# Delta rule of a hybrid block: N and A formed from the raw channel-major keys, the key scale folded into the decay tile

## The chip, the cores and the metric

The kernel runs on one core of one Trainium2 chip. The metric is the device time of one execution in microseconds. The kernel before took 1391.35 us, the median of 3 runs (1386.46 to 1392.39).

## The reference, cut to what matters

One layer on x of 1024 tokens by 1024 channels, all in float32. After an rmsnorm and one projection, two mixers work side by side: forgetting attention (FoX, 8 heads of 64) and a gated delta rule (GDN, 4 heads of 128). Their outputs are joined, projected by w_out, normed and added; a squared-relu MLP of width 4096 follows. The part that the change touches is the delta rule:

```python
cq = cq * lax.rsqrt(jnp.sum(cq * cq, axis=-1, keepdims=True) + EPS) * GDN_HEAD_DIM ** -0.5
ck = ck * lax.rsqrt(jnp.sum(ck * ck, axis=-1, keepdims=True) + EPS)
beta = jax.nn.sigmoid(gb)
decay = exp(where(incl, gc[..., :, None] - gc[..., None, :], -inf))
m = where(strict, einsum("bhncd,bhnkd->bhnck", k * beta, k) * decay, 0.0)
t_inv = triangular_solve(eye + m, eye, lower, unit_diagonal)
u = t_inv @ (v * beta)
w = t_inv @ (k * beta * exp(gc))
a_intra = einsum("bhncd,bhnkd->bhnck", q, k) * decay
# then a scan over the chunks: v_new, o, and the new state
```

## The kernel before, in words

The kernel has three parts one after the other: the input projection with its causal convolutions, the mixers, and w_out with the MLP. The change lies in the mixers.

For each of the 4 delta-rule heads p there is a preparation (`list_prep`) and a scan over 8 chunks of 128 tokens (`list_scan`). The FoX heads are cut in 64 tiles of 128 queries (`list_fox`), whose items lie between those of the delta rule on every engine. A preparation works on two halves g (0 and 1) of 4 chunks each. Its steps are "fills": each fill is one PSUM bank of four 128x128 blocks written by TensorE, either by four transposes (`four_turned`) or by four products (`four_products`), and then read by ScalarE or VectorE. The fills of all heads rotate through 3 banks (`NFILL_BANKS`), so that a fill can't begin before the fill three places ahead of it has been read.

The keys come from DRAM channel-major (`c_raw["k"]`, `c_first["k"]` for head 0: 128 channels by 1024 tokens). The path of the keys of one half before the change is:

1. fill "k": TensorE turns the raw keys to token-major in PSUM.
2. ScalarE squares them (L1815), VectorE sums (L2349) and adds the epsilon (L2351): "mean". GpSimd raises the mean to a power (L2864), for the values.
3. VectorE forms `k_scale` = beta / mean (L2362, L2364) and writes the scaled keys `kn` = keys * `k_scale` (L2366): "scale". Then it writes `kbg` (L2375) from the same bank: "kb". `kbg` has one buffer for each half, so "kb" of head p waits for the fill "W" of head p-1, which reads it.
4. fill "knT": TensorE turns `kn` back to channel-major; ScalarE copies it to `knT` (L1841).
5. fill "N": products of `knT` with the raw keys; VectorE multiplies by -1 and the decay tile (L2448) into `n_low`. fill "A": products of `knT` with the raw queries, times the decay tile (L2452), into `a_t`.
6. When both halves of `n_low` are there, the SyncE queue gathers the 16x16 diagonal blocks through DRAM (L1454, L1457), VectorE inverts them ("lane", L2388 to L2427), the queue scatters them back (L1462 on), and three levels of fills X, TX and XR build the inverse. Fills W and U multiply it into the keys and the values, and the scan of the head can begin.

The decay tile (128 by 1024 floats) is made for each head: a broadcast load of the gate row (L1364), two ScalarE reads of it (L1796, L1797), a GpSimd product with the mask (L2869), and 8 ScalarE exponentials (L1803). The next head's row is loaded once both N and both A have been read. GpSimd also makes `kd` (L2879, from `kn`), `qdT` (L2885), `z_tok` (L2918), the powers of the norms (L2903, L2905), and for each FoX tile `q_lo` (L2895), which the scores of that tile wait for.

The order of the items on each engine is worked out before the kernel is built, by `plan()`: a list scheduler in plain Python that has a cost for every item (`pe_cost`, `act_cost`, `dve_cost`, `pool_cost`, `sp_cost`), what each item follows (`fill_follows`, `dve_follows`, `pool_follows` and so on) and a fixed beginning (`BEGUN`). It always takes the item that can start first, and of those that start together the one with the longest way to the end. On the chip each engine works its list off in order. An item added or taken out can so move many others on all five engines. The planner lets a fill start only when the other things its reader waits for are done.

Of the kernel before, what the change touches and what calls it, by code (L numbers as in the profile page):

```python
# [14 lines left out]
P = 128  # L15
# [15 lines left out]
LEVELS = 7  # L31
# [59 lines left out]
ACT_READS = ("mask", "fv", "z", "knT", "W")  # L91
# [30 lines left out]
def list_prep(p):  # L122

    fills = [(p, what, g, 0) for what in ("fv", "k", "q", "v", "z", "knT", "N", "A", "W", "U") for g in range(2)]
    fills += [(p, "XR", g, BASE - 1) for g in range(2)]
    for lev in range(BASE, LEVELS):
        for g in range(2):
            fills += [(p, "X", g, lev), (p, "XR", g, lev)] + ([(p, "TX", g, lev)] if lev < LEVELS - 1 else [])
    for name in fills + [(0, "mask", 0, 0)] * (p == 0):
        what, lev = name[1], name[3]  # L130
        to("pe", "fill", name)
        if what in ("k", "q"):
            to("act", "square", name)
            to("dve", "mean", name)
            if what == "k":
                to("pool", "power", name)
                to("dve", "scale", name)
                to("dve", "kb", name)
        else:
            to("act" if read_by_act(what, lev) else "dve", "read", name)  # L140
        if what == "knT":
            to("pool", "kd", name)
    to("act", "gl", p)
    to("pool", "decay", p)
    to("act", "decay", p)
    to("pool", "qd", p)
    to("pool", "z", p)
    to("sp", "gather", p)
    to("sp", "scatter", p)
    for part in range(LANE_PARTS):  # L150
        to("dve", "lane", p, part)
    if p >= 1:
        for what in ("fv", "k", "q", "v", "z", "g"):
            to("sp", "load", what, p)
# [81 lines left out]
def pe_cost(item):  # L236

    kind = item[0]
    if kind == "fill":
        what, lev = item[1][1], item[1][3]  # L240
        if what == "mask":
            return 0.33
        return 0.44 if what in ("fv", "k", "q", "v", "z", "knT") or (what == "XR" and lev < LEVELS - 1) else 0.9
    if kind == "scores":
        blocks = FOX_TILES[item[1]][2] + 1
        return 0.066 + sum(2 * max(0.112, 0.057 * min(4, blocks - b)) for b in range(0, blocks, 4))
    if kind in ("turn", "pv"):
        return (0.11 if kind == "turn" else 0.224) * blocks_of(*item[1:])
    return 0.224 if kind == "scan_v" else 0.672 if item[2] else 0.448
# [25 lines left out]
def pool_cost(item):  # L275

    return {"power": 1.02, "decay": 2.37, "kd": 1.05, "qd": 2.37, "queries": 0.47, "z": 2.4, "tail_power": 1.02, "w_out": 2.37}[item[0]]
# [40 lines left out]
def fill_follows(p, what, g, lev):  # L318

    before = [reader((p, w, g, l)) for w, l in {  # L320
        "N": [("knT", 0)], "A": [("knT", 0)], "X": [("TX", lev - 1)] * (lev > BASE), "TX": [("X", lev), ("XR", lev - 1)],
        "XR": [] if lev < BASE else [("TX", lev)] if lev < LEVELS - 1 else [("X", lev), ("XR", lev - 1)],
        "W": [("XR", LEVELS - 1), ("k", 0)], "U": [("XR", LEVELS - 1), ("v", 0)]}.get(what, [])]
    if what in ("fv", "z", "k", "q", "v"):
        before.append(("sp", "load", what, p))
    elif what == "A":
        before.append(("sp", "load", "q", p))
    elif what == "knT":
        before += [("dve", "scale", (p, "k", g, 0))] + [fill(p - 1, "A", g, 0)] * (p >= 1)
    elif (what, lev) in (("X", BASE), ("XR", BASE - 1)):  # L330
        before += [("sp", "scatter", p)] + [fill(p - 1, w, g, 0) for w in "WU"] * (p >= 1)
    elif what == "X" or (what == "XR" and lev < LEVELS - 1):
        before.append(fill(p, "TX", g, lev - 1 if what == "X" else lev))
    return before + [fill(p, what, 0, lev)] * (g if what in ("fv","k","q","z","v") else 0)


def pe_follows(kind, n, c=0):

    if kind == "fill":
        return fill_follows(*n)  # L340
    if kind == "scores":
        return [("pool", "queries", n)] + [("dve", "k_lo", n // NT)] * (n % NT == 0) + [("dve", "max", n - 1)] * (n >= 1)
    if kind == "turn":
        before = FOX_CHUNKS[max(FOX_CHUNK[(n, c)] - 1, 0)]
        return [("act", "exp", n)] + [(copied_by(*before), "copy") + before] * ((n, c) != (0, 0))
    if kind == "pv":
        before = [(copied_by(n, c), "copy", n, c), reader((FOX_TILES[n][0], "fv", 1, 0))]
        return before + ([("pe", "pv", n, 0)] if c else [("act", "out", n - 1)] * (n >= 1))
    if kind == "scan_v":
        return [("dve", "state", n, c - 1), ("act", "o", n, c - 1), reader((n, "W", c // HT, 0)), reader((n, "U", c // HT, 0))]  # L350
    before = [reader((n, w, c // HT, 0)) for w in "UA"] + [("pool", "qd", n), ("pool", "kd", (n, "knT", 1, 0))]
    if c:
        return before + [("dve", "v_new", n, c)] + [("pe", "scores", NT - 1)] * ((n, c) == (0, NCHUNK - 1))
    return before + last_state(n - 1) + [("act", "o", n - 1, NCHUNK - 1)] * (n >= 1)


def act_follows(kind, n=None, c=0):

    if kind == "square":
        p, what, g, _ = n  # L360
        if what == "k":
            return [fill(*n)] + [("pool", "kd", (p - 1, "knT", g, 0))] * (p >= 1)
# [33 lines left out]
def dve_follows(kind, n, c=0):  # L396

    if kind in ("mean", "scale", "kb"):
        p, what, g, _ = n
        if kind == "mean":  # L400
            return [("act", "square", n)] + [("dve", "read", (p - 1, "v", g, 0)), ("dve", "scale", (p - 1, "k", g, 0))] * (what == "k" and p >= 1)
        return [("dve", "mean" if kind == "scale" else "scale", n)] + [fill(p - 1, "W", g, 0)] * (kind == "kb" and p >= 1)
    if kind == "lane":
        return [("dve", "lane", n, c - 1) if c else ("sp", "gather", n)]
    if kind == "read":
# [4 lines left out]
        elif what in ("N", "A"):  # L410
            before += [("act", "decay", p)] + ([fill(p - 1, "X", g, LEVELS - 1)] * (p >= 1) if what == "N" else last_state(p - 2))
# [27 lines left out]
def pool_follows(kind, n):  # L439
# [5 lines left out]
    if kind == "kd":  # L445
        return [("dve", "scale", (n[0], "k", n[2], 0)), fill(*n)] + last_state(n[0] - 2)
# [7 lines left out]
def sp_follows(kind, what, n=0):  # L454
# [12 lines left out]
    return [fill(n - 1, {"k": "N", "q": "A"}.get(what, what), 1, 0)] + [("pool", "qd", n - 1)] * (what == "q")  # L467
# [99 lines left out]
POOL_PREP = numbered_of("pool", "power", "decay", "kd", "qd")  # L567
# [115 lines left out]
def build(nc, x, pre_mix_norm, w_in, fox_f_bias, fox_out_norm, gdn_conv_w, gdn_a_log,  # L683
# [7 lines left out]
    with ExitStack() as ctx:  # L691
# [124 lines left out]
        knT = [placed(f"knT{g}", at, [P, 4, P]) for g, at in enumerate((192448, 206784))]  # L816
# [468 lines left out]
        def _(sp):  # L1285
# [60 lines left out]
            def load_c(kind, h):  # L1346
                if h >= 1:
                    sp.wait_ge(filled, FILL[(h - 1, {"k": "N", "q": "A"}.get(kind, kind), 1, 0)])
# [272 lines left out]
        def _(act):  # L1621
# [184 lines left out]
            def square(name):  # L1806
# [5 lines left out]
                if what == "k":  # L1812
                    if p >= 1:
                        act.wait_ge(pool_prep, POOL_PREP[("kd", (p - 1, "knT", g, 0))])
# [6 lines left out]
            def read(name):  # L1821
# [10 lines left out]
                dst = {"fv": v_tok[s][:, four, :], "z": z_tok[s][:, four, :], "knT": knT[g][:, :, :],  # L1832
# [365 lines left out]
        def _(dve):  # L2198
# [145 lines left out]
            def norm_mean(name):  # L2344
# [9 lines left out]
                dve.wait_ge(norm_sum, NORM_SUM[("mean", name)])  # L2354
                nc.vector.tensor_scalar(q_eps[:, p % 2, 4 * g:4 * g + 4], q_sums[:, :], EPS, GDN_DIM * GDN_DIM * EPS, ALU.add, ALU.mult).then_inc(dve_prep, 1)

            def norm_scale(name):
# [3 lines left out]
                dve.wait_ge(dve_prep, DVE_PREP[("mean", name)])  # L2361
                nc.vector.reciprocal(k_scale[:, g, :], means[:, g, :]).then_inc(scale_step, 1)  # L2362
# [66 lines left out]
            def read(name):  # L2429
# [14 lines left out]
                elif what == "N":  # L2444
                    if p >= 1:
                        dve.wait_ge(filled, FILL[(p - 1, "X", g, LEVELS - 1)])
                    dve.wait_ge(act_prep, ACT_PREP[("decay", p)])
                    nc.vector.scalar_tensor_tensor(out=n_low[:, g, :, :], in0=src, scalar=-1.0, in1=decay[:, four, :],  # L2448
                                                   op0=ALU.mult, op1=ALU.mult).then_inc(dve_prep, 1)
                elif what == "A":  # L2450
                    dve.wait_ge(act_prep, ACT_PREP[("decay", p)])
# [47 lines left out]
            def mean(tail):  # L2499
# [3 lines left out]
                if what == "gdn":  # L2503
                    dve.wait_ge(gdn_square_done, n * NCHUNK + (half + 1) * HT)
                    nc.vector.tensor_tensor(gdn_ms[:, cols], gdn_ss[:, cols], q_eps[:, n % 2, cols], ALU.add).then_inc(tail_mean, 1)
# [291 lines left out]
        def _(pool):  # L2797
# [73 lines left out]
            def k_decayed(name):  # L2871
# [4 lines left out]
                pool.wait_ge(filled, FILL[name])  # L2876
                if p >= 2:
                    pool.wait_ge(scan_done, (p - 1) * NCHUNK)
                nc.gpsimd.tensor_tensor(kd[p % 2][:, four, :], kn[:, g, :, :], wide(gates_all[:, G_REST, p, four], P), ALU.mult).then_inc(pool_prep, 1)  # L2879

# [41 lines left out]
            for item in ORDER["pool"]:  # L2922
# [3 lines left out]
                elif kind == "decay":  # L2926
                    decay_mask(n)
                elif kind == "kd":
# [111 lines left out]
        def _(pe):  # L3040
# [98 lines left out]
            def prep(name):  # L3139
# [32 lines left out]
                elif what == "knT":  # L3172
                    after_dve("scale", "k", g, 0)
                    four_turned(f, lambda i: kn[:, g, i, :])
                elif what == "N":
                    after_act("knT", g, 0)
                    raw = (c_raw if p else c_first)["k"]
                    four_products(f, lambda i: knT[g][:, i, :], lambda i: raw[:, tok[i]])
                elif what == "A":
                    after_act("knT", g, 0)  # L3180
                    four_products(f, lambda i: knT[g][:, i, :], lambda i: c_raw["q"][:, tok[i]])
# [101 lines left out]
            def scan_second(h, c):  # L3283

                s, n = h % 2, h * NCHUNK + c
                if c == 0:

                    pe.wait_ge(dve_prep, DVE_PREP[("read", (h, "U", 0, 0))])
                    pe.wait_ge(pool_prep, max(POOL_PREP[("qd", h)], POOL_PREP[("kd", (h, "knT", 1, 0))]))
# [232 lines left out]
```

## Time and profile before

| | us |
|---|---|
| median of 3 runs | 1391.35 |
| profiled execution | 1389.17 |
| its span, first to last instruction | 1386.7 |
| TensorE busy | 1319.8 |
| VectorE busy | 918.7 |
| ScalarE busy | 645.6 |
| GpSimd busy | 540.9 |

The span is the time between the first and the last instruction; the profiled execution took 2.47 us more than that. Busy times of the engines overlap, and each is a mean over three parts with different limits. A busy TensorE isn't one at its peak: a matmul counts until its modelled end.

### The profile page before, as it was taken

Reading aid. Unit: us, or ns where it says so; the run is one execution under the profiler, and the core shown is the slowest. Engines: PE = TensorE matmul, PEld = TensorE weight load, DVE = VectorE, ACT = ScalarE, POOL = GpSimd, SP = SyncE. Lnnn points to the kernel's source line nnn. Section 1 sums busy time; section 2 is a strip of 40 time slices with the busy share of each in tenths; the row PEclk is TensorE's granted clock in tenths of the full one; section 3 lists DMA queues with packets and bytes.
Section 4 is the critical chain, followed back from the end, with each engine's and each line's share of the span. In section 5 each row is a group of like instructions: output and inputs, shape, how many; then the busy total and the mean of one; then the engine's idle time right before and its main releaser. Section 6 shows DMA issues by size and latency. Waiting matters only on the chain.

```text
span 1386.7 us, 19443 instructions
## 1 busy us (share of the span) xinstructions
PE 1319.8 (95%) x6800; PEld 1111.0 (80%) x6800; DVE 918.7 (66%) x1506; ACT 645.6 (47%) x1381; POOL 540.9 (39%) x438
## 2 busy tenths in 40 slices
PE   5999999998899999998999899999999999999996
PEld 4778888887798989887887688888887888888885
DVE  6977776657678786753557996555555674444567
ACT  6655333446657576663335332333322444445453
POOL 3742333214423332334013776656563354441001
PEclk9999999999899999998999999999999999999999
DMA  6233223346514142043222455434535983334433
GB/s 198 62 123 121 78 85 112 122 152 204 162 33 123 46 119 57 9 107 92 82 85 77 122 188 167 149 125 143 167 137 192 374 283 99 99 94 159 157 93 150
DMA packets 145319, 178.58 MB, mean 129 GB/s; under 512 B 19852, under 2 KB 92860, under 8 KB 145224
## 3 DMA queue, kind: packets, MB, share of 16 engines
q1 hardware_dynamic: 145224, 177.35, 40.0%
q8 instruction: 55, 0.90, 0.3%
q14 instruction: 40, 0.33, 0.1%
HBM read 124.31 MB, written 53.00 MB: 128 GB/s over the span
## 4 chain that ended last, share of the span: by engine, by line
PE 78%; DVE 11%; DMA 3%; issue 3%; ACT 3%; POOL 1%; SPq 1%; DVEq 0%; ACTq 0%; POOLq 0%
PE ps L3425 7%; PE ps L3427 7%; PE ps L3426 7%; PE ps L3438 6%; PE ps L3439 6%; PE ps L3440 6%; PE ps L3082 6%; PE ps L3084 6%; PE ps L3083 6%; PE ps L3131 5%; PE ps L3266 3%; PE ps L3377 2%; PE ps L3379 2%; PE ps L3378 2%; PE ps L3252 2%
## 5 line engine op out<-in xcount | busy, mean ns | idle before, releaser
L3438 PE MATMUL ps<-db_hi,da_hi 128*128 128x512 f32 x448 | 175.3, 391 | 4.0 <-DVE db_lo L2718 4.0
L3439 PE MATMUL ps<-db_lo,da_hi 128*128 128x512 f32 x448 | 174.4, 389 | 0.0
L3440 PE MATMUL ps<-db_hi,da_lo 128*128 128x512 f32 x448 | 174.3, 389 | 0.0
L2716 DVE TENSOR_TENSOR da_lo<-a_raw,da_hi 128x512 fp32r<-128x512 f32 x112 | 85.6, 764 | 121.0 <-ACT da_hi L2124 120.9
L2124 ACT ACTIVATE da_hi<-a_raw 128x512 fp32r<-128x512 f32 x112 | 70.7, 631 | 159.1 <-PE ps L3440 138.1
L3425 PE MATMUL ps<-bt_hi,ring_hi 128*128 128x512 f32 x320 | 127.2, 397 | 5.1 <-DVE ring_lo L2638 5.1
L3427 PE MATMUL ps<-bt_hi,ring_lo 128*128 128x512 f32 x320 | 126.1, 394 | 0.0
L3426 PE MATMUL ps<-bt_lo,ring_hi 128*128 128x512 f32 x320 | 125.7, 393 | 0.0
L3082 PE MATMUL ps<-i_bt_hi,i_ring_hi 128*128 128x512 f32 x280 | 111.0, 396 | 3.0 <-DVE i_ring_lo L2216 1.6
L3084 PE MATMUL ps<-i_bt_hi,i_ring_lo 128*128 128x512 f32 x280 | 110.3, 394 | 0.0
L3083 PE MATMUL ps<-i_bt_lo,i_ring_hi 128*128 128x512 f32 x280 | 110.0, 393 | 0.0
L3438 PEld LDWEIGHTS ps<-db_hi,da_hi 128*128 128x128 f32 x448 | 84.1, 188 | 24.9 <-DVE db_lo L2718 7.7
L3440 PEld LDWEIGHTS ps<-db_hi,da_lo 128*128 128x128 f32 x448 | 84.1, 188 | 17.7
L3439 PEld LDWEIGHTS ps<-db_lo,da_hi 128*128 128x128 f32 x448 | 84.1, 188 | 17.0
L2948 POOL TENSOR_TENSOR o_rs<-o_ms,halves 128x1 f32<-128x1 f32 x24 | 16.5, 687 | 206.2 <-DVE o_ms L2616 94.7
L2023 ACT ACTIVATE ring_hi<-s_w 128x512 fp32r<-128x512 f32 x64 | 40.3, 632 | 120.6 <-PE ps L3427 118.9
L2718 DVE TENSOR_TENSOR db_lo<-wd,db_hi 128x512 fp32r<-128x512 f32 x112 | 88.7, 792 | 0.0
L2895 POOL TENSOR_TENSOR q_lo<-q,q_hi 128x128 fp32r<-128x128 f32 x64 | 31.1, 486 | 129.9 <-ACT q_hi L1860 127.3
L3266 PE MATMUL ps<-v_tok,probs_t 128*128 128x64 f32 x576 | 80.4, 278 | 1.4 <-ACT probs_t L1849 1.2
L3266 PEld LDWEIGHTS ps<-v_tok,probs_t 128*128 128x128 f32 x576 | 76.6, 202 | 2.8 <-ACT probs_t L1849 2.0
L3425 PEld LDWEIGHTS ps<-bt_hi,ring_hi 128*128 128x128 f32 x320 | 60.8, 190 | 18.5 <-DVE ring_lo L2638 5.6
L3427 PEld LDWEIGHTS ps<-bt_hi,ring_lo 128*128 128x128 f32 x320 | 60.6, 189 | 14.3
(382 smaller groups left out, 3447.7 us busy)
## 6 DMA issues: line engine op xcount, KB each, us to landing
a_raw<-act_dram SPq DMA_DIRECT2D x112, 256.0 KB, 2.6
act_dram<-s_act SPq DMA_DIRECT2D x64, 256.0 KB, 2.2
wd<-in_w_down_dram SPq DMA_DIRECT2D x15, 1024.0 KB, 7.7
act_dram<-c SPq DMA_DIRECT2D x48, 256.0 KB, 4.8
w_top<-in_w_up_dram SPq DMA_DIRECT2D x18, 512.0 KB, 4.2
w_bot<-in_w_up_dram SPq DMA_DIRECT2D x16, 512.0 KB, 5.4
i_top<-in_w_in_dram SPq DMA_DIRECT2D x14, 512.0 KB, 3.9
i_bot<-in_w_in_dram SPq DMA_DIRECT2D x14, 512.0 KB, 5.2
```

The lines of the kernel that those rows point to most:

```text
L2716: nc.vector.tensor_tensor(da_lo[s][:, :], a_raw[n % 4][:, :], da_hi[s][:, :].bitcast(F32), ALU.subtract).then_inc(d_lo_ready, 1)
L2718: nc.vector.tensor_tensor(db_lo[s][:, :], d_moving(n), db_hi[s][:, :].bitcast(F32), ALU.subtract).then_inc(d_lo_ready, 1)
L3082: nc.tensor.matmul(acc, i_ring_hi[r][:, k, :], b_hi[:, k, :], start=(first and k == 0), stop=False, skip_group_check=True)
L3083: nc.tensor.matmul(acc, i_ring_hi[r][:, k, :], b_lo[:, k, :], start=False, stop=False, skip_group_check=True)
L3084: last = nc.tensor.matmul(acc, i_ring_lo[r][:, k, :], b_hi[:, k, :], start=False, stop=(k == HK - 1), skip_group_check=True)
L3266: last = nc.tensor.matmul(fox_o(i)[:, 0:FOX_DIM], probs_t[n % 2][:, kb - 4 * c, :], v_tok[h % 2][:, kb, hh * FOX_DIM:(hh + 1) * FOX_DIM], ...
L3425: nc.tensor.matmul(acc, ring_hi[r][:, k, :], b_hi[:, k, :], start=(first and k == 0), stop=False, skip_group_check=True)
L3426: nc.tensor.matmul(acc, ring_hi[r][:, k, :], b_lo[:, k, :], start=False, stop=False, skip_group_check=True)
L3427: last = nc.tensor.matmul(acc, ring_lo[r][:, k, :], b_hi[:, k, :], start=False, stop=(k == HK - 1), skip_group_check=True)
L3438: nc.tensor.matmul(acc, da_hi[s][:, cols], db_hi[s][:, :], start=start, stop=False, skip_group_check=True)
L3439: nc.tensor.matmul(acc, da_hi[s][:, cols], db_lo[s][:, :], start=False, stop=False, skip_group_check=True)
L3440: return nc.tensor.matmul(acc, da_lo[s][:, cols], db_hi[s][:, :], start=False, stop=stop, skip_group_check=True)
```

## The change

N is formed as raw keys times raw keys, and A as raw keys times raw queries. The factor `k_scale`, which belongs to the key token and thus to the partition of both results, goes into the decay tile: a new GpSimd item "scaled" multiplies the whole tile (128x1024) by `k_scale`, broadcast along the free axis, after the exponentials and after "scale" of both halves. The reads of N and of A wait for it in place of the exponentials. The fills "knT", their two ScalarE copies for each head and the `knT` buffers are gone. `kd` no longer waits for a fill. The load of the raw keys of the next head now waits for the fills k, N and A of this one, since A reads the raw keys too. "scale" of head p waits for "scaled" of head p-1, as `k_scale` has one buffer. For the same reason of reuse, "mean" of q of head p waits for the gated tail mean of head p-2 on VectorE, and that tail mean waits for its own head's "mean".

```diff
@@ -121,7 +121,7 @@
 def list_prep(p):
-    fills = [(p, what, g, 0) for what in ("fv", "k", "q", "v", "z", "knT", "N", "A", "W", "U") for g in range(2)]
+    fills = [(p, what, g, 0) for what in ("fv", "k", "q", "v", "z", "N", "A", "W", "U") for g in range(2)]
@@ -136,13 +136,13 @@
+                to("pool", "kd", name)
-        if what == "knT":
-            to("pool", "kd", name)
+    to("pool", "scaled", p)
@@ -318,15 +318,13 @@
 def fill_follows(p, what, g, lev):
-        "N": [("knT", 0)], "A": [("knT", 0)], "X": [("TX", lev - 1)] * (lev > BASE), "TX": [("X", lev), ("XR", lev - 1)],
+        "X": [("TX", lev - 1)] * (lev > BASE), "TX": [("X", lev), ("XR", lev - 1)],
-    elif what == "A":
-        before.append(("sp", "load", "q", p))
-    elif what == "knT":
-        before += [("dve", "scale", (p, "k", g, 0))] + [fill(p - 1, "A", g, 0)] * (p >= 1)
+    elif what in ("N", "A"):
+        before += [("sp", "load", w, p) for w in ("k", "q")[:1 if what == "N" else 2]]
@@ -348,7 +346,7 @@
-    before = [reader((n, w, c // HT, 0)) for w in "UA"] + [("pool", "qd", n), ("pool", "kd", (n, "knT", 1, 0))]
+    before = [reader((n, w, c // HT, 0)) for w in "UA"] + [("pool", "qd", n), ("pool", "kd", (n, "k", 1, 0))]
@@ -359,7 +357,7 @@
-            return [fill(*n)] + [("pool", "kd", (p - 1, "knT", g, 0))] * (p >= 1)
+            return [fill(*n)] + [("pool", "kd", (p - 1, "k", g, 0))] * (p >= 1)
@@ -398,8 +396,10 @@
-            return [("act", "square", n)] + [("dve", "read", (p - 1, "v", g, 0)), ("dve", "scale", (p - 1, "k", g, 0))] * (what == "k" and p >= 1)
-        return [("dve", "mean" if kind == "scale" else "scale", n)] + [fill(p - 1, "W", g, 0)] * (kind == "kb" and p >= 1)
+            return [("act", "square", n)] + [("dve", "read", (p - 1, "v", g, 0)), ("dve", "scale", (p - 1, "k", g, 0))] * (what == "k" and p >= 1) \
+                + [("dve", "tail_mean", ("gdn", p - 2, g))] * (what == "q" and p >= 2)
+        return [("dve", "mean" if kind == "scale" else "scale", n)] + [fill(p - 1, "W", g, 0)] * (kind == "kb" and p >= 1) \
+            + [("pool", "scaled", p - 1)] * (kind == "scale" and p >= 1)
@@ -408,7 +408,7 @@
-            before += [("act", "decay", p)] + ([fill(p - 1, "X", g, LEVELS - 1)] * (p >= 1) if what == "N" else last_state(p - 2))
+            before += [("pool", "scaled", p)] + ([fill(p - 1, "X", g, LEVELS - 1)] * (p >= 1) if what == "N" else last_state(p - 2))
@@ -443,7 +443,9 @@
-        return [("dve", "scale", (n[0], "k", n[2], 0)), fill(*n)] + last_state(n[0] - 2)
+        return [("dve", "scale", n)] + last_state(n[0] - 2)
+    if kind == "scaled":
+        return [("act", "decay", n)] + [("dve", "scale", (n, "k", g, 0)) for g in range(2)]
@@ -464,7 +466,7 @@
-    return [fill(n - 1, {"k": "N", "q": "A"}.get(what, what), 1, 0)] + [("pool", "qd", n - 1)] * (what == "q")
+    return [fill(n - 1, what, 1, 0)] + [fill(n - 1, w, 1, 0) for w in {"k": "NA", "q": "A"}.get(what, "")] + [("pool", "qd", n - 1)] * (what == "q")
 def follows(key):
@@ -564,7 +566,7 @@
-POOL_PREP = numbered_of("pool", "power", "decay", "kd", "qd")
+POOL_PREP = numbered_of("pool", "power", "decay", "scaled", "kd", "qd")
@@ -813,7 +815,6 @@
-        knT = [placed(f"knT{g}", at, [P, 4, P]) for g, at in enumerate((192448, 206784))]
@@ -1345,7 +1346,8 @@
             def load_c(kind, h):
-                    sp.wait_ge(filled, FILL[(h - 1, {"k": "N", "q": "A"}.get(kind, kind), 1, 0)])
+                    for what in {"k": "kNA", "q": "qA"}.get(kind, kind):
+                        sp.wait_ge(filled, FILL[(h - 1, what, 1, 0)])
@@ -2352,6 +2354,8 @@
+                if p >= 2:
+                    dve.wait_ge(tail_mean, MEAN[("gdn", p - 2, g)])
             def norm_scale(name):
@@ -2359,6 +2363,8 @@
+                if p >= 1:
+                    dve.wait_ge(pool_prep, POOL_PREP[("scaled", p - 1)])
@@ -2444,11 +2450,11 @@
-                    dve.wait_ge(act_prep, ACT_PREP[("decay", p)])
+                    dve.wait_ge(pool_prep, POOL_PREP[("scaled", p)])
-                    dve.wait_ge(act_prep, ACT_PREP[("decay", p)])
+                    dve.wait_ge(pool_prep, POOL_PREP[("scaled", p)])
@@ -2502,6 +2508,7 @@
+                    dve.wait_ge(dve_prep, DVE_PREP[("mean", (n, "q", half, 0))])
@@ -2873,10 +2880,17 @@
-                pool.wait_ge(filled, FILL[name])
+
+            def decay_scaled(p):
+
+                pool.wait_ge(act_prep, ACT_PREP[("decay", p)])
+                for g in range(2):
+                    pool.wait_ge(dve_prep, DVE_PREP[("scale", (p, "k", g, 0))])
+                nc.gpsimd.tensor_tensor(decay[:, :, :], decay[:, :, :], wide(k_scale[:, :, :].rearrange("p g t -> p (g t)"), P),
+                                        ALU.mult).then_inc(pool_prep, 1)
             def q_grown(p):
@@ -3169,16 +3185,15 @@
-                elif what == "knT":
-                    after_dve("scale", "k", g, 0)
-                    four_turned(f, lambda i: kn[:, g, i, :])
-                    after_act("knT", g, 0)
+                    pe.wait_ge(c_loaded["k"], 16 * (p + 1))
-                    four_products(f, lambda i: knT[g][:, i, :], lambda i: raw[:, tok[i]])
+                    four_products(f, lambda i: raw[:, tok[i]], lambda i: raw[:, tok[i]])
-                    after_act("knT", g, 0)
-                    four_products(f, lambda i: knT[g][:, i, :], lambda i: c_raw["q"][:, tok[i]])
+                    pe.wait_ge(c_loaded["k"], 16 * (p + 1))
+                    pe.wait_ge(c_loaded["q"], 16 * (p + 1))
+                    raw = (c_raw if p else c_first)["k"]
+                    four_products(f, lambda i: raw[:, tok[i]], lambda i: c_raw["q"][:, tok[i]])
@@ -3286,7 +3301,7 @@
-                    pe.wait_ge(pool_prep, max(POOL_PREP[("qd", h)], POOL_PREP[("kd", (h, "knT", 1, 0))]))
+                    pe.wait_ge(pool_prep, max(POOL_PREP[("qd", h)], POOL_PREP[("kd", (h, "k", 1, 0))]))
```

## Rows read from the trace of the kernel before

**Rows 1.** Windows: start and end, length, busy us by engine (instructions), clock, DMA share.
```profile
0.00:325.00 325.00, 305.38 (x1330) 247.15 (x1331) 239.82 (x303) 153.16 (x221) 115.28 (x91) 1.00 0.38 117
325.00:640.00 315.00, 289.86 (x2276) 270.75 (x2277) 225.17 (x624) 204.25 (x671) 118.07 (x123) 0.94 0.33 95
640.00:1386.00 746.00, 724.55 (x3197) 593.10 (x3195) 453.72 (x581) 288.13 (x490) 307.50 (x225) 0.99 0.44 148
```

**Rows 2.** Timeline of the mixers' end: start, us, engine, line, operation, tiles, wait before.
```profile
634.31 0.22 ACT L1881 ACTIVATE mixed_half<-ps 128x64 f32<-128x64 f32 x1 [1.47 <-PE ps L3266]
636.38 0.35 DVE L2495 SCALAR_TENSOR_TENSOR state<-state,g_last,ps 128x128 f32<-128x128 f32 x1
```

**Rows 3.** A window of 5 us while the blocks of the last head are inverted.
```profile
580.00:585.00 5.00, 2.19 (x11) 2.11 (x12) 3.78 (x10) 2.64 (x9) 1.37 (x2) 0.82 0.07 16
```

**Rows 4.** Waits from 320 to 645 us: waiter, releaser, total us, times, longest.
```profile
POOL q_lo L2895 <- ACT q_hi L1860: 127.3, 46, 16.3
```

**Rows 5.** Tiles kn and knT, and timeline: what the change takes away.
```profile
L3136 PE MATMUL ps<-const,kn x32: 272/273/473, 326.2 to 563.5; 128*128 128x128 f32 x32
466.26 0.47 PEld L3136 LDWEIGHTS ps<-const,kn 128*128 128x128 f32 x4
L1841 ACT ACTIVATE knT<-ps x8: 575/597/621, 328.1 to 563.9; 128x512 f32<-128x512 f32 x8
```

**Rows 6.** Tiles decay and n_low, and timeline: the nearest GpSimd product; reads and products of N.
```profile
L2869 POOL TENSOR_TENSOR decay<-decay,const x4: 2344/2357/2824, 328.1 to 500.0; 128x1024 f32<-128x1024 f32 x4
L2448 DVE SCALAR_TENSOR_TENSOR n_low<-ps,decay x8: 680/692/693, 340.8 to 566.2; 128x512 f32<-128x512 f32 x8
467.81 0.97 PEld L3131 LDWEIGHTS ps<-c_raw_k,knT 128*128 128x128 f32 x8
```

**Rows 7.** Timeline, head 0: exponentials, qdT, second read of N, gather.
```profile
332.33 2.44 ACT L1803 ACTIVATE decay<-decay,gates_all 128x128 f32<-128x128 f32 x8
332.94 2.38 POOL L2885 TENSOR_TENSOR qdT<-qdT,c_raw_q 128x1024 f32<-128x1024 f32 x1
343.33 0.69 DVE L2448 SCALAR_TENSOR_TENSOR n_low<-ps,decay 128x512 f32<-128x512 f32 x1
344.29 1.80 SPq L1454 DMA_DIRECT2D n_dram<-n_low  x4
```

**Rows 8.** Tile kn and timeline, head 1: both kn, second kn, second read, gather.
```profile
L2366 DVE TENSOR_TENSOR kn<-ps,k_scale x2: 691/691/691, 400.5 to 406.4; 128x512 f32<-128x512 f32 x2
406.38 0.69 DVE L2366 TENSOR_TENSOR kn<-ps,k_scale 128x512 f32<-128x512 f32 x1
413.93 0.69 DVE L2448 SCALAR_TENSOR_TENSOR n_low<-ps,decay 128x512 f32<-128x512 f32 x1 [0.25 <-PE ps L3131]
414.70 3.32 SPq L1454 DMA_DIRECT2D n_dram<-n_low  x6
```

**Rows 9.** Tiles kn and n_low in the window 480 to 540 and before, head 2.
```profile
L2366 DVE TENSOR_TENSOR kn<-ps,k_scale x2: 691/691/691, 464.9 to 478.8; 128x512 f32<-128x512 f32 x2
L1454 SPq DMA_DIRECT2D n_dram<-n_low x8: 319/430/435, 484.9 to 488.1; - x8
```

**Rows 10.** Tile kn and timeline, head 3: both kn, second kn, gather.
```profile
L2366 DVE TENSOR_TENSOR kn<-ps,k_scale x2: 691/691/691, 541.0 to 562.0; 128x512 f32<-128x512 f32 x2
561.95 0.69 DVE L2366 TENSOR_TENSOR kn<-ps,k_scale 128x512 f32<-128x512 f32 x1
566.99 4.44 SPq L1454 DMA_DIRECT2D n_dram<-n_low  x8
```

**Rows 11.** Timeline from 501 us: small VectorE operations beside GpSimd products.
```profile
501.12 1.23 DVE L2509 SCALAR_TENSOR_TENSOR fox_rr<-row_sum 128x4 f32<-128x4 f32 x1
502.27 2.37 POOL L2885 TENSOR_TENSOR qdT<-qdT,c_raw_q 128x1024 f32<-128x1024 f32 x1
502.38 2.29 DVE L2511 TENSOR_TENSOR fox_ms<-fox_ss,fox_rr 128x4 f32<-128x4 f32 x1
504.77 0.31 DVE L2511 TENSOR_TENSOR fox_ms<-fox_ss,fox_rr 128x4 f32<-128x4 f32 x1
```

More of the change, by code:

```diff
@@ L90 @@
 NFILL_BANKS = 3
-ACT_READS = ("mask", "fv", "z", "knT", "W")
+ACT_READS = ("mask", "fv", "z", "W")
 def read_by_act(what, lev):
@@ L242, in pe_cost @@
             return 0.33
-        return 0.44 if what in ("fv", "k", "q", "v", "z", "knT") or (what == "XR" and lev < LEVELS - 1) else 0.9
+        return 0.44 if what in ("fv", "k", "q", "v", "z") or (what == "XR" and lev < LEVELS - 1) else 0.9
     if kind == "scores":
@@ L275, in pool_cost @@
 def pool_cost(item):
-    return {"power": 1.02, "decay": 2.37, "kd": 1.05, "qd": 2.37, "queries": 0.47, "z": 2.4, "tail_power": 1.02, "w_out": 2.37}[item[0]]
+    return {"power": 1.02, "decay": 2.37, "scaled": 2.37, "kd": 1.05, "qd": 2.37, "queries": 0.47, "z": 2.4, "tail_power": 1.02, "w_out": 2.37}[item[0]]
 def sp_cost(item):
@@ L1813, in square @@
                     if p >= 1:
-                        act.wait_ge(pool_prep, POOL_PREP[("kd", (p - 1, "knT", g, 0))])
+                        act.wait_ge(pool_prep, POOL_PREP[("kd", (p - 1, "k", g, 0))])
                     nc.scalar.activation(kn[:, g, :, :], bank4(FILL[name] - 1), ACT.Square).then_inc(act_prep, 1)
@@ L1830, in read @@
                     return
-                dst = {"fv": v_tok[s][:, four, :], "z": z_tok[s][:, four, :], "knT": knT[g][:, :, :],
+                dst = {"fv": v_tok[s][:, four, :], "z": z_tok[s][:, four, :],
                        "XR": r_inv[:, g, :, :], "W": w_all[s][:, four, :]}[what]
@@ L2927, in _ @@
                     decay_mask(n)
+                elif kind == "scaled":
+                    decay_scaled(n)
                 elif kind == "kd":
```

## The prediction

> **What bounds the kernel now.** I read the busy times by stretch first. The mixers take 315 us of the span, the MLP after them 746 [rows 1]. In the MLP TensorE is busy 724.55 of 746 us and the change touches nothing there, so whatever the mixers gain or lose passes to the end one for one. In the mixers every engine has room: TensorE is busy 290 of 315 us by modelled ends, VectorE 225, ScalarE 204, GpSimd 118 [rows 1]. So I looked next for what they wait for. While the diagonal blocks of the last head are inverted, TensorE works 2.19 us of 5 and its clock falls to 0.82 on the mean [rows 3]: it has only FoX to do then, and nothing of the delta rule can start. That is a chain, not a full engine.
>
> The chain is the delta rule's from head to head: "kb" of head p needs the fill W of head p-1, the gather needs both N of head p, and W of head p needs the inverse that comes out of the gather. The starts of the gathers show its period: 344.29, 414.70, 484.9 and 566.99 us [rows 7 to 10], which is 70.4, 70.2 and 82.1 us for one head, and 69 from the last to the last state [rows 2]. FoX fills the holes and ends with it: its last output is read at 634.31, the last state is written at 636.38 [rows 2]. So the edit counts where it changes the stretch from "scale" of the second half to the gather, and FoX has about 2.1 us of room over the whole stage.
>
> **What goes.** 32 transposes of kn, at 0.47 us for four at TensorE's pace, are 8 x 0.47 = 3.8 us of TensorE; 8 copies to knT of 0.6 us are 4.8 us of ScalarE [rows 5]. As load these count for nothing in my sum, because neither engine is full; what they are worth is their place in the chain, which is counted next. N and A keep the same number of products.
>
> **What comes.** One GpSimd product of 128x1024 per head. The trace doesn't show this one, but the mask product on the same tile took 2.357 us [rows 6]; it also reads two tensors of that size, while the new one reads a broadcast of 8 columns. I take 2.36, with 2.34 and 2.82 as ends, four of them.
>
> **The stretch before the gather, old against new.** Old: transposes, copy, products, read, one after the other for the second half, each queued behind FoX items. New: 2.36 for the product, then two reads of N of 0.69 [rows 6], as the first half must wait as well. If the N fills stand in PSUM by then this is 2.36 + 1.38 = 3.74 us. If the planner puts them behind the product (it holds a fill back until its reader's other needs are met), it is 2.36 + 2 x 0.97 + 0.69 = 4.99 us [rows 6]. By head:
> - Head 0. The exponentials end at 334.77, but GpSimd is in qdT until 335.32 [rows 7]. The gather could start at 339.1 to 340.3, against 344.29: 4.0 to 5.2 us earlier.
> - Head 1. kn ends at 407.07, so 410.8 to 412.1 against 414.70 [rows 8]: 2.6 to 3.9 earlier.
> - Head 2. kn starts at 478.8 and ends at 479.5, so 483.2 to 484.5 against 484.9 [rows 9]: 0.4 to 1.7 earlier.
> - Head 3. kn ends at 562.64, so 566.4 to 567.6 against 566.99 [rows 10]: 0.6 earlier to 0.6 later. There the old path was already as short as the new one.
>
> The sum is 6.4 to 11.4 us; the middle is 8.9. From it I take three things. The two reads come in a row on a VectorE that is busy 71% of the stage [rows 1], so about one other operation of 0.69 us stands ahead in each head: 2.8 us. Half of head 0's gain, 2 us, goes back, since its gather then meets the loads of the stage's start (with the DMA queue in order, and the lanes waiting for landings); the ends are 0 and the full 4.6. And 1 us for what the new product holds up, below. That leaves 8.9 - 2.8 - 2 - 1 = 3.1 us.
>
> **What is moved.** The load of the next raw keys waits for A instead of N; head 2 doesn't scale its keys until 50 us after the gather of head 1 [rows 8, 9], so nothing. If it is issued ahead of the gather in the SyncE queue, the gather waits for A's fills too, up to 2 x 0.97 = 1.9 us in heads 0 to 2; head 3 has no such load. N and A lean on "scaled" and hold up to three PSUM banks while they wait; FoX has its own banks, and the fills v and z that would come next are not on the chain: nothing to 1.9 us. The new waits of q's mean and of the gated tail mean are for things finished long before. kd starts earlier, being free of a fill: nothing, since the scan starts much later.
>
> **What the new product can hold up.** First GpSimd's own queue: q_lo of a FoX tile behind it waits up to 2.36 us. GpSimd waited 127.3 us for q_hi in 46 of these [rows 4], so it has time, but not always at that moment. Second VectorE. Beside the product for qdT, an operation on 128x4 took 2.29 us and ended at 504.67, as the GpSimd product ended at 504.64; the same line took 0.31 us right after [rows 11]. An operation that stalls so delays whatever is queued behind it, by at most 2.36 us; the reads of N behind it lose nothing, because they wait for the product anyway. Between nothing and 4 x 2.36 = 9.4 us I take 1, near the low end, since only the small norm operations show it. The Trainium skill ("SBUF — State Buffer", section "Who interferes with whom") says that a VectorE instruction with both inputs in SBUF contends with a GpSimd instruction that reads SBUF, the later one being blocked for the whole of the other. The trace agrees, by the 2.29 us above. Taken alone it would speak against this change, and it is part of the rival on the slow side.
>
> **Sum.** 1389.17 - 3.1 = 1386.1 us in the terms of the profiled execution, which is 2.18 us below the median of the runs and 2.47 above its span. For the median I forecast 1388 us, a gain of 0.2%. This case's own range is 1380 (all of the 11.4) to 1391 (nothing left).
>
> **The rivals.**
> 1. The order is drawn anew, for the better. The planner takes whatever can start first, so 8 fills and 8 copies fewer and 4 products more shift every list. The gap between kn of the two halves is 5.9 us in head 1 (400.5 to 406.4), 13.9 in head 2 and 21.0 in head 3 [rows 8 to 10], and head 3 is the one whose period is 82.1. If it fell to the 70.2 of head 2, that gives 11.9 us; with the 3.1 it is 1391.35 - 15 = 1376. For it: the lag is a matter of order and not of work. Against it: nothing in the edit aims at it.
> 2. The same for the worse. If head 1 lagged as head 3 does, 21.0 - 5.9 = 15.1 us come on top: 1403; half of it 1396.
> 3. Slower through GpSimd. The product lies in the queue before q_lo and in VectorE's way, and FoX, not the delta rule, becomes what ends last. It decides once FoX has fallen back by more than its 2.1 us of room [rows 2]. Four times 2.36 less 2.1 are 7.3 us, with the chain's gain worth nothing: 1398.6. For it: FoX and the delta rule end so close together. Against it: GpSimd's long waits for q_hi, and FoX is the filler elsewhere.
> 4. The shorter stretch turns into waiting (for the lanes on VectorE, for the DMAs, or for FoX work that must be done in any case): 1391.
>
> **How the numbers follow.** The forecast 0.45, rival 1 0.15, rival 2 0.10, rival 3 0.13, rival 4 0.17. A difference under 0.5%, 7 us, can't be told from no change here, so faster means under 1384.4 and slower over 1398.3. Faster: all of rival 1 and three tenths of the forecast's range, 0.15 + 0.14 = 0.29. Slower: half of rival 2 and most of rival 3, 0.05 + 0.08 = 0.13. The rest, 0.58, is no change that can be told. The range from 1377 to 1400 leaves out the far ends of rivals 1 and 2.
>
> **What would show it.** The gather of head 0 should start 3 to 5 us earlier, that of head 3 should start 3.7 to 5.0 us after the end of its second kn (4.35 before); the new product at 2.3 to 2.8 us, four times; no transposes of kn; the end of the mixers about 3 us earlier and the MLP as long as before. The forecast is wrong if periods of heads change by more than their stretches before the gather do (then the order did it), if FoX's last output comes well after the last state, or if small VectorE operations of 2 us stand beside the new product at many places.

## The result, and the profile after

The changed kernel takes 1401.45 us (1399.57 to 1402.65, 4 runs) against 1390.84 for the kernel before (1386.46 to 1392.39): 1.0085 of its time (95% interval 1.0066 to 1.0103), slower by 0.85%, where 0.2% faster was forecast. The profiled execution is 1402.65 us with a span of 1400.5, which is 13.8 more than before. It is at the upper end of its runs and the profiled execution before 1.7 us below its median, so the two profiles differ by about 3 us more than the medians, which differ by 10.6.

The windows of the kernel after, cut where its mixers end (start and end, length, busy us by engine, clock, DMA share):

```profile
0.00:325.00 325.00, 305.64 (x1332) 247.59 (x1332) 239.71 (x303) 153.38 (x221) 116.36 (x91) 1.00 0.37 117
325.00:654.00 329.00, 294.17 (x2239) 273.78 (x2239) 224.83 (x622) 202.16 (x663) 128.03 (x127) 0.90 0.31 91
654.00:1400.00 746.00, 724.44 (x3200) 593.72 (x3198) 452.67 (x584) 287.82 (x490) 306.87 (x225) 0.99 0.45 148
```

Against [rows 1] the first and the last part are the same to 0.3 us of TensorE; all of the loss is in the mixers, 315 us before and 329 after. The end of the mixers in the timeline, beside [rows 2]:

```profile
645.65 0.22 ACT L1883 ACTIVATE mixed_half<-ps 128x64 f32<-128x64 f32 x1
652.01 0.35 DVE L2501 SCALAR_TENSOR_TENSOR state<-state,g_last,ps 128x128 f32<-128x128 f32 x1 [1.22 <-PE ps L3323]
```

The last state is 15.6 us later than before, of which 13.8 reach the end of the span; FoX's last output is 11.3 us later. FoX now ends 6.4 us ahead of the delta rule, so the chain of the delta rule is what got longer. The gathers of its heads, in the timeline of the SyncE queue:

```profile
345.30 3.70 SPq L1456 DMA_DIRECT2D n_dram<-n_low  x8
414.71 3.77 SPq L1456 DMA_DIRECT2D n_dram<-n_low  x8
480.97 3.62 SPq L1456 DMA_DIRECT2D n_dram<-n_low  x8
576.42 4.92 SPq L1456 DMA_DIRECT2D n_dram<-n_low  x8
```

Against [rows 7 to 10] they are 1.0 us later, the same, 3.9 us earlier and 9.4 us later. Between the third and the fourth the kernel before needed 82.1 us, this one 95.5. By their starts the pieces of these 13.4 us are: gather to the store of the inverted blocks -0.3, store to scatter +6.6, scatter to the end of the second kn of head 3 +1.6, from there to the gather +5.4. These are lengths on the clock and not yet prices: the experiments show how little of the second reached the end. From the fourth gather to the last state it is 75.6 us instead of 69.4, another 6.2. Four places are worth a look.

**The store of the inverted blocks waits for loads.** The SyncE queue from the third gather on:

```profile
485.70 0.45 SPq L1459 DMA_DIRECT2D lane_n<-n_dram  x1
486.19 0.58 SPq L1366 DMA_DIRECT2D decay<-gate_dram  x1
486.94 0.34 SPq L1355 DMA_DIRECT2D c_raw_k<-proj_dram  x1
487.38 1.09 SPq L1376 DMA_DIRECT2D kk_raw<-proj_dram  x2
488.57 1.24 SPq L1385 DMA_DIRECT2D q<-proj_dram  x2
489.85 0.61 SPq L1395 DMA_DIRECT2D cum_row<-gate_dram  x1
490.56 0.39 SPq L1355 DMA_DIRECT2D c_raw_v<-proj_dram  x1
491.11 0.36 SPq L1355 DMA_DIRECT2D c_raw_q<-proj_dram  x1
491.56 0.39 SPq L1355 DMA_DIRECT2D c_raw_z<-proj_dram  x1
495.61 0.47 SPq L1464 DMA_DIRECT2D t_dram<-lane_t  x1
504.19 3.63 SPq L1473 DMA_DIRECT2D t_low<-t_dram  x8
```

Those are six loads in ten DMAs (gate row, k, a FoX half head, v, q, z). The kernel before has two of them between the gather and the store:

```profile
490.13 0.59 SPq L1364 DMA_DIRECT2D decay<-gate_dram  x1
490.83 0.36 SPq L1353 DMA_DIRECT2D c_raw_q<-proj_dram  x1
499.86 0.47 SPq L1462 DMA_DIRECT2D t_dram<-lane_t  x1
501.80 3.63 SPq L1471 DMA_DIRECT2D t_low<-t_dram  x8
```

From store to scatter it is 8.6 us instead of 1.9: the store is 4.2 us earlier and the scatter 2.4 us later. The waits of the queue name the landing (waiter, releaser, total, times, longest):

```profile
SPq L1473 <- DMA t_dram<-lane_t: 8.0, 1, 8.0
```

**TensorE stands still behind the same loads, and its clock falls.** Windows of 5 us of the kernel after:

```profile
490.00:495.00 5.00, 2.83 (x24) 2.42 (x22) 4.90 (x10) 1.87 (x8) 4.60 (x3) 0.94 1.02 277
495.00:500.00 5.00, 1.51 (x6) 1.14 (x6) 2.49 (x6) 2.52 (x7) 0.20 (x1) 0.50 1.03 309
500.00:505.00 5.00, 2.90 (x12) 2.53 (x12) 0.35 (x1) 1.19 (x3) 0.00 (x0) 0.50 0.41 156
505.00:510.00 5.00, 4.42 (x25) 4.01 (x24) 2.88 (x11) 3.46 (x13) 3.77 (x3) 0.69 0.20 36
```

The timeline of ScalarE and TensorE, in brackets what they waited for:

```profile
496.13 1.06 ACT L1790 ACTIVATE k_split<-kk_raw 128x1024 fp32r<-128x1024 f32 x1 [4.09 <-DMA kk_raw<-proj_dram]
497.49 0.66 PE L3267 MATMUL ps<-const,probs 128*128 128x128 f32 x2 [3.17 <-ACT probs_t L1851]
502.10 1.09 PE L3152 MATMUL ps<-const,c_raw_q 128*128 128x128 f32 x4 [3.09 <-DMA c_raw_q<-proj_dram]
```

In the same 20 us the kernel before has 5.00, 4.14, 4.26 and 3.40 us of TensorE. Here it waits 3.2 us for a copy of ScalarE, which itself stood 4.1 us for the FoX keys among the loads, and then 3.1 us for the queries of head 3, with the scan and FoX queued behind that fill; its clock is at 0.50, the 1.2 GHz level, for 10 us, after 5 us of which it worked 2.83.

**The stretch before the gather is long.** From the end of the second kn to the gather it is 7.50, 7.84 and 9.79 us in heads 1 to 3, against 7.63, 5.40 and 4.35 before. VectorE, TensorE and GpSimd in head 3:

```profile
565.94 0.69 DVE L2372 TENSOR_TENSOR kn<-ps,k_scale 128x512 f32<-128x512 f32 x1
566.97 1.90 POOL L2892 TENSOR_TENSOR decay<-decay,k_scale 128x1024 f32<-128x1024 f32 x1
567.43 1.46 DVE L2516 SCALAR_TENSOR_TENSOR fox_rr<-row_sum 128x4 f32<-128x4 f32 x1
571.45 1.11 PE L3147 MATMUL ps<-c_raw_k 128*128 128x128 f32 x8
572.60 0.69 DVE L2454 SCALAR_TENSOR_TENSOR n_low<-ps,decay 128x512 f32<-128x512 f32 x1
573.21 1.69 DVE L2512 TENSOR_TENSOR gdn_ms<-gdn_ss,q_eps 128x4 f32<-128x4 f32 x1
573.74 1.06 PE L3147 MATMUL ps<-c_raw_k 128*128 128x128 f32 x8
575.67 0.68 DVE L2454 SCALAR_TENSOR_TENSOR n_low<-ps,decay 128x512 f32<-128x512 f32 x1
```

The product is done at 568.87. The first N fill needs raw keys that landed long before, and a free bank: three fills ahead of it stands the fill k of the second half, and VectorE reads that one last in "kb":

```profile
570.37 0.69 DVE L2381 TENSOR_TENSOR kbg<-ps,gates_all 128x512 f32<-128x512 f32 x1
```

"kb" stands behind a FoX maximum in VectorE's list and ends at 571.06. So the fill starts at 571.45, 2.6 us after the product, by two things: its place behind the scores of a FoX tile, and the bank, which wasn't free much earlier. The second starts 2.3 us after the first, and its read stands behind norm operations. In heads 0 to 2 the fill A of the first half stands between the two N fills in TensorE's list as well. Over the four heads the product takes:

```profile
L2892 POOL TENSOR_TENSOR decay<-decay,k_scale x4: 1898/1914/2921, 334.3 to 567.0; 128x1024 f32<-128x1024 f32 x4
```

**Behind the last gather the clock is lower.** The first 10 us after the start of the last scatter, before and after, and the first X product of head 3 in each:

```profile
584.56:594.56 10.00, 10.00 (x63) 9.38 (x62) 4.95 (x19) 5.88 (x22) 2.74 (x5) 0.73 0.08 8
594.32:604.32 10.00, 9.99 (x43) 8.82 (x44) 5.15 (x21) 5.09 (x24) 3.42 (x5) 0.50 0.08 9
592.43 1.11 PE L3131 MATMUL ps<-t_low,n_low 128*128 128x128 f32 x8
604.90 2.02 PE L3147 MATMUL ps<-t_low,n_low 128*128 128x128 f32 x8
```

TensorE is busy throughout in both, mostly with FoX, but from the start of the scatter to the X product it is 10.6 us instead of 7.9. In the run tiny below, which has the same lists, the clock is 0.84 in these 10 us and the X product comes after 7.9. So 2.7 of the 6.2 us go with the clock; where the rest arises no run here isolates.

### The profile page after: what moved, and what is told of

Read it like the earlier page. It is cut to its first block, busy times and chain, and to the rows that moved or that the text cites. A ratio compares the mean times of both kernels' runs of the same rounds, so it can differ in the third digit from the quotient of the medians.

```text
span 1400.5 us, 19392 instructions
## 1 busy us (share of the span) xinstructions
PE 1324.2 (95%) x6768; PEld 1115.1 (80%) x6768; DVE 917.2 (65%) x1506; ACT 643.4 (46%) x1373; POOL 551.3 (39%) x442
## 4 chain that ended last, share of the span: by engine, by line
PE 81%; DVE 9%; DMA 3%; issue 2%; ACT 2%; SPq 2%; POOL 0%; DVEq 0%; ACTq 0%
PE ps L3440 7%; PE ps L3442 7%; PE ps L3441 7%; PE ps L3453 6%; PE ps L3455 6%; PE ps L3454 6%; PE ps L3098 6%; PE ps L3100 6%; PE ps L3099 6%; PE ps L3147 5%; PE ps L3281 3%; PE ps L3392 2%; PE ps L3394 2%; PE ps L3393 2%; PE ps L3267 2%
## 5 line engine op out<-in xcount | busy, mean ns | idle before, releaser
L3281 PE MATMUL ps<-v_tok,probs_t 128*128 128x64 f32 x576 | 83.7, 286 | 1.0 <-ACT sq_fox L1886 0.6
L3281 PEld LDWEIGHTS ps<-v_tok,probs_t 128*128 128x128 f32 x576 | 80.4, 211 | 2.0 <-issue 1.1
```

Of the source, the lines that this page charges most:

```text
L3281: last = nc.tensor.matmul(fox_o(i)[:, 0:FOX_DIM], probs_t[n % 2][:, kb - 4 * c, :], v_tok[h % 2][:, kb, hh * FOX_DIM:(hh + 1) * FOX_DIM], ...
```

## The experiments

Theory ORDER: the arithmetic is worth little, and the time is lost in where the planner's new draw puts fills and loads. Rival PRODUCT (or ARITHMETIC): the GpSimd product and what it holds up cost the time. Ratios below are to runs of the kernel before on the same chip.

**oldorder.**

```diff
 ORDER = plan()          # of the kernel before
+# fills and reads "knT" taken out of the lists;
+# ("scaled", (p, g)) put in ahead of kd of the same half (head 0: behind qdT);
+# load k of p+1 behind the gather of p
+nc.gpsimd.tensor_tensor(decay[:, four, :], decay[:, four, :], wide(k_scale[:, g, :], P), ALU.mult)
```

> The new arithmetic in the old order: the lists of the kernel before, with the knT items taken out and the product put in as two halves, each right ahead of kd of its half (head 0: behind qdT), the load of the next raw keys behind the gather. Theory ORDER (the 10.6 us are the newly drawn order: fills of N behind FoX items, and loads that meet the scatter of head 2): 1388 to 1393, as the kernel before or a little under. Rival PRODUCT (GpSimd's product in the way of VectorE and of its own queue): 1397 to 1402, since there are still four times 2 us and more of it.

Measured: 1.0024 (1.0006 to 1.0043), in the range of ORDER. With the new arithmetic and the old lists 0.24% is left of 0.85%. The gathers are at 344.16, 415.28, 484.08 and 568.09, within 1.1 us of [rows 7 to 10]; store to scatter in head 2 takes 1.9 us again; the stretches are 7.34, 5.00 and 4.03 us.

**tiny.**

```diff
-nc.gpsimd.tensor_tensor(decay[:, :, :], decay[:, :, :], wide(k_scale..., P), ALU.mult)
+nc.gpsimd.tensor_tensor(decay[:, :, 0:1], decay[:, :, 0:1], wide(k_scale..., 1), ALU.mult)
```

> The changed kernel, same order, with the product cut from 1024 columns to 8 (one for each chunk), all waits kept; the scale so is missing in N and A, and N gets the constant factor -0.001 in its place. Theory PRODUCT: 4 products of 1.9 to 2.9 us go, with the VectorE operations that they held up (1.3 us in head 3): 1394 to 1397. Theory ORDER: the N fills still stand where they stand in TensorE's list, so 1399 to 1401.

Measured: 1.0081 (1.0052 to 1.0110), as the changed kernel. The products now take 0.21 to 1.23 us, and the stretches are 7.51, 7.83 and 9.19: all but unchanged. The product isn't what they wait for. PRODUCT falls, as far as these runs resolve: by the interval, 4 us of it could hide.

**spmove.**

```diff
+_held = [("load", what, 3) for what in "kvz"]   # taken out of the SyncE list and
+_sp[_at:_at] = _held                            # put back right behind ("scatter", 2)
```

> The changed kernel with three loads (k, v and z of head 3, 0.5 MB each) moved behind the scatter of head 2 in the SyncE queue, nothing else. Theory ORDER, part loads: the store of the inverted blocks of head 2 lands after 2 us instead of 8.0, and 6 us less come through: 1395. Rival: the 6 us are hidden by what the engines have to do by then: 1400 to 1401.5, with the store landing early all the same.

Measured: 1.0068 (1.0041 to 1.0094), which can't be told from the 1.0085. Every list but SyncE's is the same here. The scatter of head 2 came at 500.30, 3.9 us earlier, the first X product at 507.50 instead of 511.90; but the XR transposes stand behind FoX items in TensorE's list and came at 516.73 instead of 518.03, and the first W of head 2 was read at 544.68 instead of 544.75. The gain was hidden, as the rival had it: from store to scatter 4.9 us went, and from the third gather to the fourth 1.0. A part of the reason may lie on VectorE, which no run tests. VectorE's and GpSimd's timeline of this run:

```profile
504.50 2.37 POOL L2881 TENSOR_TENSOR decay<-decay,const 128x1024 f32<-128x1024 f32 x1
505.31 4.77 DVE L2531 SCALAR_TENSOR_TENSOR mixed_half<-mixed_half,fox_ms,fox_norm_row 128x64 f32<-128x64 f32 x4
507.66 2.35 POOL L2904 TENSOR_TENSOR qdT<-qdT,c_raw_q 128x1024 f32<-128x1024 f32 x1
```

Four small norms ended at 510.08, with the second of two GpSimd products (510.01), and the next FoX maximum stood behind them; in the changed kernel the same four took 0.98 us, with a product beside only their first 0.3 us. Both products are old ones; the order put them beside the norms.

**early.**

```diff
+# the planner may start fills N and A when both kn and the exponentials are done
+if name[1] in ("N", "A"):
+    held = [k for k in held if k[1] != "scaled"] + [scale of both halves, exponentials]
```

> The changed kernel with the planner told that fills N and A may start once the keys are scaled and the exponentials done, without waiting for the product. Theory ORDER, part fills: the stretch from the last kn to the gather falls from 7.5 to 9.8 us to 4.5 to 6 in heads 1 to 3, which is 6 to 9 us in all, if the order drawn is otherwise no worse: 1392 to 1396. Rival PRODUCT: the stretch keeps 7 us or more: 1399 to 1402.

Measured: 0.9974 (0.9959 to 0.9989), faster than the kernel before and than the 1392 to 1396 expected. The stretches are 6.95, 6.04 and 5.95 us, the gathers 3.3, 6.5 and 7.6 us earlier than before, the last 0.4 later. So the fills have a part in it. But head 1 kept 6.95 us where 4.5 to 6 were expected, and the planner drew all lists anew (332 of the 461 places on TensorE hold another item), which a lucky draw could do as well. Between the third and the fourth gather the gain goes, beside the loads again:

```profile
491.32 0.47 SPq L1467 DMA_DIRECT2D t_dram<-lane_t  x1
500.81 3.64 SPq L1476 DMA_DIRECT2D t_low<-t_dram  x8
```

**neworder.**

```diff
 ORDER = plan()          # of the kernel after, without "scaled"
+ORDER["pe"].insert(place of fill N, ("fill", (p, "knT", g, 0)))
+ORDER["act"].insert(..., ("read", (p, "knT", g, 0)))
```

> The other corner: the old arithmetic (turned keys, knT copies, no GpSimd product) in the lists of the changed kernel, with each knT fill right ahead of its N fill. Theory ORDER: slow as the changed kernel, 1399 to 1405, by up to 2 us of more hops in the stretch before each gather. Rival ARITHMETIC (the new product and the held keys cost the time): back to 1389 to 1392.

Measured: 1.0129 (1.0103 to 1.0156), 1407.38 us, above the changed kernel and above the 1399 to 1405 expected. The stretches are 10.35, 10.74 and 10.67 us. With oldorder this fills the square: the old order gives 1 (old arithmetic) and 1.0024 (new), the new order 1.0129 and 1.0085. The order costs 0.6 to 1.3%; the arithmetic is worth -0.4% in the new order, where the two intervals touch, and +0.2% in the old.

**early_hold.**

```diff
-return [fill(n - 1, what, 1, 0)] + ...
+return [("sp", "scatter", n - 1)] * (what in "kvz" and n == 3) + [fill(n - 1, what, 1, 0)] + ...
```

> The kernel early (fills N and A free to start before the product), with the loads k, v and z of head 3 held in the SyncE queue until the scatter of head 2; all other lists are the same. In early the store of the inverted blocks of head 2 was followed by the scatter only 9.5 us later, against 1.9 where nothing is in its way. Theory ORDER, part loads: the scatter comes 5 to 7 us earlier; if that comes through to the end, 1379 to 1382. Rival: it is hidden, as it was after the same move in the changed kernel (W of head 2 came no earlier there): 1384 to 1386.

Measured: 0.9943 (0.9926 to 0.9959), the fastest of all, 1382.78 us against 1390.36; the interval of early ends where this one does, at 0.9959. The other lists are nearly those of early, not quite as expected: besides SyncE's, 25 places changed, nearly all in heads 0 and 1. Here a part of the move comes through:

```profile
492.63 0.47 SPq L1467 DMA_DIRECT2D t_dram<-lane_t  x1
496.01 3.64 SPq L1476 DMA_DIRECT2D t_low<-t_dram  x8
```

Store to scatter is 3.4 us instead of 9.5, the fourth gather is at 565.21 instead of 567.40, and the last state at 632.44 instead of 634.63. From the third gather to the fourth it is 86.6 us instead of 90.1, so 3.5 of the 6.1 us arrive there; the gathers before stand 1.3 to 1.7 us later than in early, and 2.2 us are left at the end.

**redraw_before and redraw_after.**

```diff
-"decay": 2.37        +"decay": 2.40        # kernel before
-"square": 0.6        +"square": 0.61       # kernel after
```

> The kernel before with one of the planner's costs changed by 1% (the GpSimd mask product, 2.37 to 2.40), nothing else; only the order of the lists changes, by the planner's own count 2.4 us for the better, in head 3. Theory ORDER (a new draw is worth several us either way, so the 10.6 us need no arithmetic): 1383 to 1395, off the kernel before by 2 us or more. Rival (the order matters little unless the work changes): 1388 to 1391.

> The changed kernel with one of the planner's costs changed by 2% (the square on ScalarE, 0.60 to 0.61), nothing else; by the planner's own count 2.8 us worse. Theory ORDER: off the changed kernel by 3 us or more, either way: 1395 to 1406. Rival: 1400 to 1402.

Measured: 0.9964 (0.9952 to 0.9976) and 1.0149 (1.0133 to 1.0164). The first is in its range, the second above the 1395 to 1406 expected. A change of 1 or 2% in one number of the planner, with the same instructions in all, moves the kernel before by -5 us and the kernel after by about +9. In redraw_before the two kn of head 3 are 12.6 us apart instead of 20.9 and its gather is 7.3 us earlier; that is the lag that rival 1 of the prediction named.

**oldorder_tiny.**

```diff
 # oldorder, with
-decay[:, four, :] ... wide(k_scale[:, g, :], P)
+decay[:, four, 0:1] ... wide(k_scale[:, g, :], 1)
```

> The kernel oldorder (new arithmetic, lists of the kernel before) with each half product cut from 512 columns to 4, waits kept; the scale is missing in N and A, with the constant factor -0.001 in N. oldorder took 0.24% (0.06 to 0.43) more than the kernel before, though its stretches before the gathers were 0.3 to 0.4 us shorter. Theory: the 8 half products cost that, by GpSimd's time and by VectorE operations that they hold: 1388 to 1390. Rival: they cost nothing in these places, as in the kernel tiny: 1391 to 1394.

Measured: 1.0002 (0.9986 to 1.0018). That is 1391.19 us, in the rival's range, on a chip where the kernel before took 1390.57; against the 1388.86 of oldorder's chip the same ratio gives 1389.1, in the theory's. Its interval overlaps that of oldorder, so that whether the half products cost 3 us there stays open.

**early_hold_all.**

```diff
-(what in "kvz" and n == 3)
+(what in "kvz" and n >= 1)
```

> early with the loads k, v and z of every head held by the planner until the scatter of the head before; the lists are drawn anew (gathers 0.6 to 0.9 us earlier by the planner's own count, end 0.6 us earlier than in early_hold). Theory ORDER: the scatter of head 0, which came 3.3 us after the store of its blocks in early_hold's profile, comes after 2 us, and the rest is as in early_hold: 1379 to 1384. Rival: the keys of head 1 now come late, or the new draw is worse elsewhere: 1385 or more.

Measured: 0.9969 (0.9955 to 0.9984), 1386.01 us, as the rival had it. The scatter of head 0 did come 2.3 us after its store, but the stretch of head 1 rose to 9.25 us: the new draw was worse elsewhere.

## Why the prediction was wrong

- **What bounds the kernel: right.** A chain from head to head, passed on nearly one for one (13.8 of 15.6 us), with the MLP unchanged.
- **The product: right, and a little dear.** 1.90 to 2.92 us, median 1.91, against 2.36 (2.34 to 2.82).
- **The stretch before the gather: this step failed.** It was put at 3.74 to 4.99 us, with 0.69 us for the queue of VectorE; measured were 7.50, 7.84 and 9.79. The working followed the data (product, two fills, two reads) and took TensorE's list as empty between them. In the lists the N fills have FoX items and the scan ahead of them, in heads 0 to 2 the fill A between them, and in head 3 a bank that was still being read. tiny shows that the product isn't the term; early points to the place of the fills, with 0.6, 1.8 and 3.8 us less in heads 1 to 3 once they may stand ahead, in lists drawn anew. In the lists of the kernel before the new arithmetic does shorten the stretch, by 0.3 to 0.4 us in each of heads 1 to 3: inside the forecast for heads 2 and 3, far from the 2.6 to 3.9 for head 1.
- **Head 0: failed.** 4.0 to 5.2 us earlier were expected; it came 1.0 later. The product ended at 336.2, the first N fill ran at 339.59 and was read at 341.34, and the second was read at 344.21.
- **"What is moved": failed.** The loads were priced at nothing, by when their data are needed. They were not priced by what they lie in front of. Head 2's gather was earlier, as forecast and for more (3.9 us); this drew six loads, against two, between it and the store of its blocks, and the way from store to scatter grew by 6.6 us. How much of that reached the end isn't shown for this kernel: spmove took 4.9 us away there and its time didn't measurably change; in early_hold 3.5 of 6.1 us came through to the next gather. Head 0's gather was said to meet loads; the same thing was not looked for in head 2.
- **What the product holds up: right in size.** In head 3 a 128x4 operation took 1.46 us and ended at 568.89, the product at 568.87. The Trainium skill's rule ("SBUF — State Buffer", "Who interferes with whom"), that a VectorE instruction with both inputs in SBUF contends with a GpSimd one that reads SBUF, is borne out here and by the 4.77 us in spmove. But taking the product away gained nothing measurable. Rival 3 didn't happen: FoX ended first.
- **The order.** Rival 2 is what happened: 13.4 us more from the third gather to the fourth. It had the right kind and nearly the right size (15.1), and a tenth of the chance; its mechanism was named wrongly, as the gap between two halves in head 1, which stayed at 5.5 us. The prediction's own sign for the order came: the period grew by 13.4 us, its stretch before the gather by 5.4. The two redraws show that a move of 5 to 9 us either way needs no change of the work at all. A range of 1377 to 1400 and 0.2% of forecast gain took the order as a side issue; it was the larger term.

## What to carry to other kernels

Where a planner writes the queues' orders, an edit is two changes: compare it in a fixed order as well as in its own (oldorder and neworder here), before it is kept or thrown away. Look at whether the items left behind in each in-order queue have moved up too: the version with earlier fills and held loads, early_hold, is 0.57% faster than the kernel before with the same arithmetic that lost 0.85%. That isn't yet a gain of the arithmetic: the kernel before gained 0.36% from a 1% change of one planner cost, and the two intervals overlap. Several draws of either kernel would have to be compared, which wasn't done. Look also at the small transfer that a moved load gets in front of, not only at its own due time.

## What the runs showed of the hardware

- A store of the inverted blocks (64 partitions) held its waiter 8.0 us when it was issued behind six loads (277 and 309 GB/s in the two windows from 490 to 500 us), and 1.4 us in the kernel before, where it stood behind two.
- GpSimd's product of 128x1024 with an operand broadcast along the free axis took 1.91 us in the middle of four, the one with a full tensor 2.36 [rows 6].
- TensorE, busy 2.83 of 5 us, ran the next 10 us at 0.50 of its clock (1.2 GHz), so that the waits were followed by slower work: after the last scatter, at 0.50 again, the same list took 10.6 us to the first X product where tiny took 7.9 at 0.84.
